# V rows fetched ten experts behind U rows in one pipeline, and summed on TensorE by diagonal matrices

## What is computed

```python
def peer_ffn(x, w_q, sub_keys, u_emb, v_emb):
    ...
    def chunk(xc):                                   # 128 tokens
        q = (xc @ w_q).reshape(PEER_CHUNK, PEER_HEADS, 2, PEER_HALF)
        s = jnp.einsum('thid,hikd->thik', q, sub_keys).astype(jnp.float32)
        ...
        top_s, pos = lax.top_k(cand, PEER_TOPK)      # 8 heads x 16 experts = 128 for a token
        eidx = jnp.take_along_axis(cidx, pos, axis=-1)
        gate = jax.nn.softmax(top_s, axis=-1)
        u = u_emb[eidx]                              # tables of 16384 rows x 1024 a layer
        hid = jax.nn.gelu(jnp.einsum('td,thkd->thk', xc, u))
        wgt = (gate * hid.astype(jnp.float32)).astype(xc.dtype)
        return jnp.einsum('thk,thkd->td', wgt, v_emb[eidx])
```

## Time and profile before

| | us |
|---|---|
| median of 3 runs | 4909.19 (4900.51 to 4909.51) |
| the profiled execution: its time | 4920.68 |
| the profiled execution: its span | 4918.8 |
| first gather of layer 0 issued, at | 711.09 |
| first gather of layer 1 issued, at | 2943.48 |
| last gather issued, at | 3762.32 |

### The profile page before, as it was taken

How to read it: one execution, slowest core, us unless ns; L and a number is a source line. 1 busy time by engine, 2 the same in 40 slices (tenths; PEclk the granted TensorE clock), 3 DMA queues, 4 the chain that set the end, 5 groups by cost and what they waited for, 6 DMA issues and landing times.

```text
span 4918.8 us, 35997 instructions
## 1 busy us (share of the span) xinstructions
PE 2853.3 (58%) x12693; PEld 2020.1 (41%) x12693; DVE 3352.0 (68%) x5718; ACT 853.5 (17%) x1543; POOL 1927.3 (39%) x1540
## 2 busy tenths in 40 slices
PE   7789973005688453028674772000002998999898
PEld 1446552003554410013542452000002986998787
DVE  1441148999666878998777448999887656655655
ACT  0130010003001000001000320000001454444443
POOL 0000015776554756776666006777774000000000
PEclk9899986555898776558897886555556997999799
DMA  6212558887989999989999228898996542545344
GB/s 225 105 43 103 179 179 308 314 293 250 341 327 364 321 386 356 328 291 359 377 378 388 76 101 302 312 337 311 367 359 253 184 167 86 185 170 180 103 154 141
DMA packets 445224, 1230.30 MB, mean 250 GB/s; under 512 B 29340, under 2 KB 65502, under 8 KB 445040
## 3 DMA queue, kind: packets, MB, share of 16 engines
q0 software_dynamic: 221184, 805.40, 45.2%
q1 hardware_dynamic: 223860, 422.60, 24.2%
HBM read 1226.84 MB, written 1.05 MB: 250 GB/s over the span
## 4 chain that ended last, share of the span: by engine, by line
PE 38%; DVE 20%; POOL 18%; DMA 14%; issue 8%; ACT 2%; SPq 0%; DVEq 0%; POOLq 0%; ACTq 0%
POOL gbuf L2382 18%; PE ps L403 16%; PE ps L680 6%; PE ps L681 6%; PE ps L682 6%; DMA gbuf<-in_peer_u,idx 6%; DVE BIG L1619 5%; DMA gbuf<-in_peer_v,idx 4%; DVE gbuf L1593 4%; DMA wbuf<-in_w_in 2%; PE ps L408 1%; DMA wbuf<-in_pool_scale 1%; PE ps L430 1%; DVE gbuf L1763 1%; DMA wbuf<-in_conv_out_w 1%
## 5 line engine op out<-in xcount | busy, mean ns | idle before, releaser
L2382 POOL DMA_INDIRECT gbuf<-in_peer_u,idx x768 | 951.9, 1239 | 1458.2 <-DVE BIG L1582 946.7
L2382 POOL DMA_INDIRECT gbuf<-in_peer_v,idx x768 | 975.3, 1270 | 377.8 <-issue 192.9
L1593 DVE CUSTOM_DVE_ANT_0 gbuf<-gbuf,BIG 128x1024 f32<-128x1024 f32 x768 | 929.8, 1221 | 208.2 <-DMA gbuf<-in_peer_u,idx 195.9
L1619 DVE SCALAR_TENSOR_TENSOR BIG<-gbuf,BIG 128x1024 f32<-128x1024 f32 x762 | 976.0, 1281 | 122.5 <-DMA gbuf<-in_peer_v,idx 104.0
L403 PE MATMUL ps<-wbuf,BIG 128*128 128x512 f32 (+1 forms) x2048 | 887.4, 594 | 84.2 <-DMA wbuf<-in_conv_out_w 28.9
L403 PEld LDWEIGHTS ps<-wbuf,BIG 128*128 128x128 f32 x2048 | 401.8, 199 | 546.1 <-issue 509.3
L1637 DVE TENSOR_TENSOR plo<-wbuf,phi 128x1024 fp32r<-128x1024 f32 (+1 forms) x344 | 401.0, 1181 | 325.0 <-ACT phi L1079 324.4
L403 PE MATMUL ps<-BIG,wbuf 128*128 128x256 f32 x1920 | 448.3, 397 | 87.3 <-DMA wbuf<-in_w_in 87.2
L403 PEld LDWEIGHTS ps<-BIG,wbuf 128*128 128x128 f32 x1920 | 383.4, 201 | 149.5 <-DMA wbuf<-in_w_in 92.9
L680 PE MATMUL ps<-XH,phi 128*128 128x256 f32 x1472 | 422.2, 287 | 18.5 <-DVE XL L1647 14.1
L681 PE MATMUL ps<-XL,phi 128*128 128x256 f32 x1472 | 421.1, 286 | 0.0
(11 more groups left out here) (336 smaller groups left out, 3582.0 us busy)
## 6 DMA issues: line engine op xcount, KB each, us to landing
wbuf<-in_w_in SPq DMA_DIRECT2D x62, 2048.0 KB
wbuf<-in_w_mod SPq DMA_DIRECT2D x24, 2048.0 KB
wbuf<-in_ffn_wg SPq DMA_DIRECT2D x20, 2048.0 KB
wbuf<-in_ffn_wu SPq DMA_DIRECT2D x20, 2048.0 KB
wbuf<-in_ffn_wd SPq DMA_DIRECT2D x16, 2048.0 KB
wbuf<-in_peer_wq SPq DMA_DIRECT2D x12, 2048.0 KB
wbuf<-in_w_in SPq DMA_DIRECT2D x14, 1536.0 KB
wbuf<-in_w_out SPq DMA_DIRECT2D x10, 2048.0 KB
```

The lines of the kernel that those rows point to most:

```text
L1593: v(ttr)(g, g, XN[:, tb, :], 1.0, 0.0, ALU.mult, ALU.add, hid[:, j:j + 1]).then_inc(dve_exp.up(T, tb, "u", j), 1)
L1619: v(stt)(ACCB, g, wv[:, j:j + 1], ACCB, ALU.mult, ALU.add).then_inc(dve_exp.up(T, tb, "v", j), 1)
L2382: g(nc.gpsimd.indirect_dma_start)(slot, None, table, bass.IndirectOffsetOnAxis(ap=idx[:, tb % 3, j:j + 1], axis=0)).then_inc(g_landed[i], 16)
```

## The change

One loop of steps replaces the runs. In step s, U row s of a sequence of tiles is gathered and used, and V row s - 10 (`LAG`), across tile borders: `AB` is A0, A1, B2, B3 as one sequence, `C` is C0, C1. The computation of the weights is done in groups of eight experts. V rows that `on_pe` names (every second in layer 0, all in layer 1) are added by TensorE: ScalarE makes `diag`, the identity times `wv[:, j]`, and two f32 matmuls diag x row accumulate in two PSUM banks that are held for a tile. The others stay on VectorE. A tile's end adds the two sums (layer 0), multiplies by the modulation row and adds to `H`. `weave` takes a rate of 2, since a step now is two gathers. The fence "ahead" becomes an `edge`, which only marks the point for SyncE.

The core of the diff (the engines' `weave` calls change alike; TensorE's are shown):

```diff
+GELU_K = 0.044715
+LAG = 10
...
-def weave(main, other):
+def weave(main, other, rate):
     n = 0.0
     for _ in main:
-        n += 1
+        n += rate
...
+        diag = Ring([small_f(128) for _ in range(4)])
...
-        def pe_experts(p, T, l, tb):
-            for _ in range(256):
+        def pe_experts(p, l, seq, s0, s1):
+            for s in range(s0, s1):
+                at = expert_at(seq, s - LAG)
+                if at:
+                    T, tb, j = at
+                    if j == 0:
+                        for n in range(2):
+                            ps.claim(p, ("acc", T, tb, n), (dve_exp, (T, tb, "acc", n)))
+                            ps.held.add(ps.where[("acc", T, tb, n)])
+                    if on_pe(T, j):
+                        g, dg = gat.of(("v", T, tb, j)), diag.of((T, tb, j))
+                        p.wait_ge(*gathered.get(("v", T, tb, j), (None, 0)))
+                        p.wait_ge(*act_exp.at(T, tb, "diag", j))
+                        for n in range(2):
+                            ins = p(mm)(ps.of(("acc", T, tb, n)), dg, g[:, n * 512:(n + 1) * 512], start=(j == 0),
+                                        stop=(j == last_on_pe(T)))
+                        ins.then_inc(pe_exp.up(T, tb, "v", j), 1)
...
                 yield
...
+        def act_experts(a, seq, s0, s1):
+            for s in range(s0, s1):
+                at = expert_at(seq, s)
+                if at and at[2] % 8 == 7:
+                    T, tb, j = at
+                    a.wait_ge(*dve_exp.at(T, tb, "poly", j // 8))
+                    a(act)(x2[:, j - 7:j + 1], x2[:, j - 7:j + 1], ACT.Tanh, scale=GELU_C * GELU_K).then_inc(
+                        act_exp.up(T, tb, "tanh", j // 8), 1)
+                at = expert_at(seq, s + 1 - LAG)
+                if at and on_pe(at[0], at[2]):
+                    T, tb, j = at
+                    dg = diag.claim(a, at, (pe_exp, (T, tb, "v", j)))
+                    a.wait_ge(*dve_exp.at(T, tb, "w", j // 8))
+                    a(act)(dg, ident[:, :], ACT.Copy, scale=wv[:, j:j + 1]).then_inc(act_exp.up(T, tb, "diag", j), 1)
...
+        def dve_experts(v, seq, s0, s1):
+            for s in range(s0, s1):
+                at = expert_at(seq, s)
+                if at:
+                    T, tb, j = at
+                    g = gat.of(("u", T, tb, j))
+                    v.wait_ge(*gathered.get(("u", T, tb, j), (None, 0)))
+                    v(ttr)(g, g, XN[:, tb, :], 1.0, 0.0, ALU.mult, ALU.add, hid[:, j:j + 1]).then_inc(
+                        dve_exp.up(T, tb, "u", j), 1)
+                    if j % 8 == 7:
+                        h8, x8 = hid[:, j - 7:j + 1], x2[:, j - 7:j + 1]
...
+                at = expert_at(seq, s - LAG)
+                if at:
+                    T, tb, j = at
+                    if not on_pe(T, j):
+                        g = gat.of(("v", T, tb, j))
...
+                            v(stt)(ACCB, g, wv[:, j:j + 1], ACCB, ALU.mult, ALU.add).then_inc(dve_exp.up(T, tb, "v", j), 1)
+                    if j == 127:
+                        dve_expert_sum(v, T, tb)
                 yield
...
+        def dve_expert_sum(v, T, tb):
+            v.wait_ge(*pe_exp.at(T, tb, "v", last_on_pe(T)))
...
+        def expert_at(seq, s):
+            return seq[s // 128] + (s % 128,) if 0 <= s < len(seq) * 128 else None
+
+        def on_pe(T, j):
+            return T == "C" or j % 2 == 0
...
-            weave(both(pe_experts(p, "A", 0, 0), pe_experts(p, "A", 0, 1)), pe_context(p))
-            fence(p, "ahead")
-            weave(both(pe_experts(p, "B", 0, 2), pe_experts(p, "B", 0, 3)), pe_ahead(p))
+            weave(pe_experts(p, 0, AB, 0, 256), pe_context(p), 2)
+            edge(p, "ahead")
+            weave(pe_experts(p, 0, AB, 256, 512 + LAG + 2), pe_ahead(p), 2)
...
         def gpsimd(g):
...
+            for seq, label in ((AB, "gather A"), (C, "gather C")):
+                after_edge(g, label)
+                for s in range(len(seq) * 128 + LAG):
+                    at = expert_at(seq, s)
+                    if at:
+                        g.wait_ge(*dve_route.at(at[0], at[1], "index", at[2] // 32))
+                        pool_gather(g, "u", *at)
+                    at = expert_at(seq, s - LAG)
+                    if at:
+                        pool_gather(g, "v", *at)
```

More of the change, by code:

```diff
@@ L655, in pe_route_scores @@
             yield from route_beats(nh)
-        def pe_experts(p, T, l, tb):
-            for _ in range(256):
+        def pe_experts(p, l, seq, s0, s1):
[16 more added lines that the diff above has]
+                    if j == 127:
+                        for n in range(2):
+                            ps.held.discard(ps.where[("acc", T, tb, n)])
+                    if j == 120:
+                        for n in range(2):
+                            pe_gate_rows(p, ("eg", T, tb, n), l, 5, n, tb // 2, act_exp, T, tb, "gate", n).then_inc(
+                                pe_exp.up(T, tb, "gate", n), 1)
                 yield
-            for n in range(2):
-                pe_gate_rows(p, ("eg", T, tb, n), l, 5, n, tb // 2, dve_exp, T, tb, "gated", n).then_inc(
-                    pe_exp.up(T, tb, n), 1)
         def pe_turn_half(p, F, half, h_of):
@@ L1621, in dve_experts @@
             for n in range(2):
                 nn = slice(n * 512, (n + 1) * 512)
-                v.wait_ge(*dve_exp.now())
-                v.wait_ge(*pe_exp.at(T, tb, n))
-                v(tt)(ACCB[:, nn], ACCB[:, nn], ps.of(("eg", T, tb, n)), ALU.mult).then_inc(
-                    dve_exp.up(T, tb, "gated", n), 1)
+                acc = ps.of(("acc", T, tb, n))
+                if T == "C":
+                    v.wait_ge(*act_exp.at(T, tb, "gate", n))
+                    v(tt)(ACCB[:, nn], acc, XN[:, tb, nn], ALU.mult).then_inc(dve_exp.up(T, tb, "acc", n), 1)
+                else:
+                    v(tt)(ACCB[:, nn], acc, ACCB[:, nn], ALU.add).then_inc(dve_exp.up(T, tb, "acc", n), 1)
@@ L1627, in dve_experts @@
+            for n in range(2):
+                nn = slice(n * 512, (n + 1) * 512)
+                if T != "C":
+                    v.wait_ge(*act_exp.at(T, tb, "gate", n))
+                    v.wait_ge(*dve_exp.at(T, tb, "acc", n))
+                    v(tt)(ACCB[:, nn], ACCB[:, nn], XN[:, tb, nn], ALU.mult).then_inc(dve_exp.up(), 1)
                 v.wait_ge(*dve_exp.now())
@@ L2100, in tensor @@
             run(pe_route_scores(p, "C", "C", 0, 0, 2))
-            weave(pe_experts(p, "C", 1, 0),
-                  both(pe_rest(p, "C", second.XT), scaled(pe_route_scores(p, "C", "C", 1), 1.0, 1)))
-            run(pe_experts(p, "C", 1, 1))
+            weave(pe_experts(p, 1, C, 0, 128),
+                  both(pe_rest(p, "C", second.XT), scaled(pe_route_scores(p, "C", "C", 1), 1.0, 1)), 2)
+            run(pe_experts(p, 1, C, 128, 256 + LAG + 2))
             fence(p, "second block")
@@ L2180, in scalar @@
             run(act_route_pass(a, "A", 0, route_before("A", 0, 0), 0, 2))
-            weave(both(act_experts(a, "A", 0), act_experts(a, "A", 1)), act_context(a))
-            fence(a, "ahead")
-            weave(both(act_experts(a, "B", 2), act_experts(a, "B", 3)), act_ahead(a))
+            weave(act_experts(a, AB, 0, 256), act_context(a), 2)
+            edge(a, "ahead")
+            weave(act_experts(a, AB, 256, 512 + LAG + 2), act_ahead(a), 2)
             fence(a, "hand over")
@@ L2279, in vector @@
             run(dve_route_pass(v, "A", 0, 0, 0, 2))
-            weave(both(dve_experts(v, "A", 0, 0), dve_experts(v, "A", 0, 1)), dve_context(v))
-            fence(v, "ahead")
-            weave(both(dve_experts(v, "B", 0, 2), dve_experts(v, "B", 0, 3)), dve_ahead(v))
+            weave(dve_experts(v, AB, 0, 256), dve_context(v), 2)
+            edge(v, "ahead")
+            weave(dve_experts(v, AB, 256, 512 + LAG + 2), dve_ahead(v), 2)
             fence(v, "hand over")
@@ L2529, in restart @@
             last.clear()
-            for ring in (ps, gat, big, tmp, wide, side, side4, narrow, sideb, sts):
+            for ring in (ps, gat, diag, big, tmp, wide, side, side4, narrow, sideb, sts):
                 ring.reset()
```

122 lines of the change are left out of this document (56 added, 66 removed).

## The result

The changed kernel takes 5000.22 us (median of 4 runs, 4987.69 to 5008.72), the kernel before beside it 4909.35: a ratio of 1.0187, 95% interval 1.0162 to 1.0212. It is slower by 91 us, where the forecast was faster by 138.

The account below looks back on a forecast made before the run. No engine bounds the kernel everywhere: VectorE or nearly in some stretches of gathers, transfers in others. Layer 0 -97, layer 1 -51, tile ends +10 make -138 us, from 4909.19 to 4771; range 4660 to 4920.

Parts of the forecast that it names:

- runs 1, 2 and 6: Layer 0 stretches of 128 gathers, VectorE the bound or nearly: 235, 236, 227 us become 205, 206, 200.
- runs 3 and 4: Layer 0 stretches of 128 gathers each, TensorE's work 485 us plus waits: 544 us becomes 545, bounds 505 and 600.
- the doubled price at 1.2 GHz: TensorE's two matmuls for a V row, 1.74 us, take twice that at the lower clock.
- runs 3, 4, 7 and 8: Layer 0 stretches of 128 gathers where the forecast fails most easily: 544 becomes 545, 484 becomes 480 us; DMA share over 0.9.
- run 5: Layer 0 stretch of 128 gathers, bound by DMA: 269 us becomes 262.
- first rival: In runs 3, 4, 7 and 8 TensorE's 222 us for V rows add in full: median 4996 us; chance 13%.
- runs 10 to 12: Layer 1's last three stretches of 128 gathers: 190, 189 and 190 us, plus 10 us after the last gather.
- second rival: TensorE stays at 1.2 GHz in layer 1, a V row costs 3.48 us: 4894 us; chance 7%.
- run 9: Layer 1's first stretch of 128 gathers: VectorE falls under 130 us, DMA sets 199 us.
- run 11: Layer 1 stretch of gathers alone, read as bound by transfers: 189 us for 128, 1.48 us each, 355 GB/s.
- third rival: Gathers alone reach 400 GB/s once GpSimd issues faster, a clean stretch is 168 us: median 4647 us; chance 8%.
- The wait of VectorE behind the dropped fence: In run 5, VectorE's 11.9 us wait for ScalarE, covered by transfers for the most part.

Follow-up runs that it names:

- the two kernels with a later turn: The changed kernel with TensorE using each V row two steps later: 5030.62 us with full matmuls, 4891.26 us with matmuls reading bfloat16 upper halves.
- the five slots: Ring of gathered rows cut from six slots to five: the kernel before takes 5047.82 us, the changed kernel 5203.06 us.
- the short form: The changed kernel with TensorE's V-row matmuls reading only the upper halves of the float32 words as bfloat16: 4860.86 us.
- the halved sum: Layer 0 V sums all on VectorE, columns 512 to 1023 left out after a tile's first row; changed layer 1: 4765.75 us (old order), 4794.85 us (new).
- twelve slots: Layer 1's ring raised from six slots to twelve: 4810.87 us with old layer 0 and changed layer 1, 4884.82 us on the kernel before.

## Why the prediction was wrong

**The step that failed** is the rule ahead of the sum: "A run lasts as long as the longest of: VectorE's work; the gathers [...]; TensorE." Its terms were close. VectorE's work in runs 1, 2 and 6 was put at 171, 200 and 185 us and is 182, 202 and 187; TensorE's in runs 3 and 4 at 485 and is 477. But the runs lasted 232, 253 and 245 us, where 205, 206 and 200 were forecast, and 575 for runs 3 and 4 together (545). Over stretches of 200 to 300 us the engines do overlap; through a ring of six slots, some 8.6 us long in layer 1, they don't. When TensorE is late by more than that, GpSimd stands, and a while later VectorE has no row: its idle time ahead of rows in layer 0 is 470 us, against 166 with no V row on TensorE. Each engine's work then adds a part of itself to the time although no engine is full.

That the V rows on TensorE cost the time is shown by taking half and all of them away; that they cost it through the slots is argued from the waits and from the two kernels with a later turn. No kernel had more slots in layer 0, and there the five slots don't tell the two orders apart. VectorE's waits for ScalarE and TensorE ahead of its other work grew too, from 115 to 216 us; which part of the loss is theirs stays open.

**The price list that the runs give for layer 0.** VectorE: 0.34 us of time for one of work, in this order. TensorE's V rows: the full and the short form differ by 459 us of their work and 119 of time, 0.26 for one. With the relief of 328 us worth 112, the pure cost of 256 rows on TensorE is 2121 - (2003 - 112) = 230 us in the full form and 110 in the short one. The straight line through both puts 0.26 x 666 = 173 us down to the matmuls and 57 to whatever else comes with a V row on TensorE: its turn in TensorE's order, the diagonals, the held banks, the tile's end. The last two are worked out, not measured apart: no run had a V row of no cost on TensorE, each layer's time carries the spread of 15 us, and with VectorE's rate of the old order the 57 would be near 90. So -112 + 173 + 57 makes the +117 that was seen.

**The price of a row** was 1.74 us from the earlier trace rows, and is 1.98 even at a granted clock of 1.00: the matmuls of the earlier trace rows stand in a long series with weights of 2 columns (128*2 in the row), the pair of a V row stands alone with weights of 128. Which of the two makes the difference, no run tells.

```profile
3702.22 1.98 PE L674 MATMUL ps<-gbuf,BIG 128*128 128x512 f32 x4 [0.56 <-DMA gbuf<-in_peer_v,idx]
```

In layer 0 it was 2.60 in the mean, as the granted clock is 0.67 to 0.70 in runs 1, 2 and 6; TensorE's work grew there from 61, 41 and 47 us to 128, 159 and 152. The forecast had named the doubled price at 1.2 GHz for these runs and left it out of the sum, since TensorE had time to spare.

**Run by run.** Of the 223 us by which layer 0 missed the forecast, 120 arose in runs 1, 2 and 6, where only the gain was looked for, 84 in runs 3, 4, 7 and 8, and 19 in run 5. The forecast asked for a DMA share over 0.9 in runs 3, 4, 7 and 8; it was 0.86, 0.89, 0.86 and 0.98. The first rival's 4996 lies 4 us from the result, and its chain is there; that the number fits is luck. It looked for 655 us in runs 3 and 4 and for 595 in runs 7 and 8, which took 575 and 533, and it left runs 1, 2 and 6 at the forecast; its 222 us of matmuls, in full, in four runs, met a pure cost of some 230 us spread over eight.

**Right:** the granted clock in layer 1, 0.97 to 1.00 in runs 10 to 12, which rules out the second rival; and that less work on VectorE shortens layer 0, shown by the halved sum. Layer 1's 775 us are near the forecast (768 by the same measure) with luck: run 9 took 223 us for 199, as VectorE had 145 us of work there for 126, and runs 10 to 12 took 185, 185 and 182 for 190, 189 and 190. Also, the better figure for layer 1's gain is 25 us, half of the forecast.

The reason given for the 190 us a run was wrong: the DMA share of 0.97 in run 11 was read as the limit of the transfers. With twelve slots a share of 1.03 goes with 408 GB/s, and a run takes 163 us. What held run 11 before was GpSimd's own issue (147 us of instructions and 38 of gaps in 189), since twelve slots did not shorten it; in the kernel after, ring and issue hold runs 10 to 12 nearly alike. The third rival had the number of the last run (168 for a clean one), and lacked what it takes: slots, and gather instructions near 0.94 us, which only that run has (0.98 in the mean).

**Small terms.** ScalarE's diagonals were put at 281 ns each from the earlier trace rows, and the operations of 128x8 at 0.19 us from the earlier trace rows:

```profile
L1093 ACT ACTIVATE BIG<-ident,BIG 128x128 f32<-128x128 f32 x512 | 188.7, 394 | 450.1 <-PE ps L674 247.6
...
3702.40 0.17 DVE L1645 SCALAR_TENSOR_TENSOR BIG<-BIG 128x8 f32<-128x8 f32 x1
```

A diagonal takes 394 ns, 189 us in all; TensorE waited for one 31 us over layer 0, most of it once (20.8). VectorE's small operations are as forecast. The wait of VectorE behind the dropped fence did not vanish under the transfers. It is four waits in layer 0 now, the longest 20.3 us:

```profile
DVE BIG L1549 <- ACT BIG L1069: 32.7, 4, 20.3
```

## What to carry to other kernels

Where engines hand rows to each other through a few slots, a sum of "the longest engine in each stretch" is too kind: price moved work at a share of its busy time (here 0.26 to 0.44), on the engine that gives and on the one that takes, plus something for each turn in an in-order engine. Before moving work off a bound, add slots where space allows: one run shows what their depth is worth. Taking one out tells less, since both orders lost about as much by it in layer 0, and layer 1 of the kernel before lost 62 us by one slot less and won 31 by six more. Here, with six more slots, the same change was worth 74 us in layer 1 (788 to 714) in place of 44 to 46.
